# Rotating the queries of the first block's attention with SBUF transfers in place of a permutation matmul

## The chip, the cores and the metric

The kernel runs on one core of one Trainium2 chip. The metric is the device time of one execution in microseconds, over repeated executions. TensorE (PE) does the matmuls, VectorE (DVE) and ScalarE (ACT) the elementwise work, SyncE (SP) issues the weight transfers, and ACT issues the smaller ones.

## The reference, cut to what matters

Two blocks run one after the other on 256 tokens of width 2048, all in float32. The first block has two layers, and each layer has a sliding-window attention with 32 query heads of width 64, 4 key/value heads and a sink logit for each head. Per layer, the part around the change computes

```
q_b = rope(q_b.reshape(b, s, 32, 64), positions)      # 32 query heads
k_b = rope(k_b.reshape(b, s, 4, 64), positions)
o_b = swa_with_sinks(q_b, k_b, v_b, sinks).reshape(b, s, 2048) * silu(z_b)

def rope(x, positions):            # half = 32
    x1, x2 = x[..., :half], x[..., half:]
    return concatenate([x1 * cos - x2 * sin, x2 * cos + x1 * sin], -1)
```

In `rope` each half of a head's 64 numbers is needed beside the other half. In the attention, token i sees the keys j with 0 <= i - j < 128, in blocks of 128 tokens; the softmax takes the sink into its denominator. The columns `q_b` and `z_b` come out of the large projection `h @ w_in`. The rest (a gated delta rule before the attention, output projections after it, and the second block) is untouched.

## The kernel before, in words

**Weights.** Every projection is computed in blocks of 128 output columns. A block's weights (128 x 2048) are streamed from HBM into one of four slots of `raw` by SP. ACT rounds each half of a block to float32r (`Wh`, line 343, `act_cast`), DVE writes the remainder (`Wl`, line 349, `dve_low`), and PE multiplies a half as 8 x 3 matmuls of 256 columns (lines 278 to 280, `pe_half`). `Wh` and `Wl` have four places, so a cast into a place waits until PE has used the half that lay there, and the casts run four halves ahead of PE. The finished tile lies in bank `G[0]` or `G[1]`, and ACT copies it out (line 1625), which counts up `tile_taken`.

**Turns.** The attention stage (`pe_swa`, `act_swa`, `dve_swa`) runs in five turns per layer, g = 0 to 4; turns 1 to 3 are one rolled loop on each engine. A turn has 16 halves, n = 0 to 15. In turns 0 to 3 these are the blocks of the gate z (4 tiles, into `zx`) and of the queries q (4 tiles, into `qx`) of kv head g. In turn 4 they are the first 8 tiles of the next projection, whose tanh goes to `gm_more`. Between the halves of turns 1 to 4 lie the softmax steps of kv head c = g - 1 (`chain` is true). There are four query tiles t = 0 to 3 per kv head, with two heads in each, on partitions 0 to 63 and 64 to 127.

**Steps of tile t.** All three engines follow one order written out by hand. PE computes the scores ahead of half 4t + 1 (lines 1539, 1540). DVE adds the window mask and finds the maxima at n = 4t + 1 (lines 1656 to 1666). ACT does four exps at n = 4t + 2 (line 1597) and the sink's exp (line 1599). DVE normalises at n = 4t + 3 (lines 1670 to 1678). PE transposes the probabilities ahead of half 4t + 4 (line 1557), ACT copies them to `PT` (line 1604), and PE multiplies by the values ahead of half 4t + 5, behind the next scores (lines 1547 to 1549). DVE multiplies by the gate (line 1686), ACT rounds (line 1591) and DVE writes the low part (line 1693) at n = 4t + 6.

**The end of a turn.** Behind half 15 PE transposes for t = 3, then waits for ACT's copy of the last query tile and multiplies the four query tiles by the constant permutation `swap`, which exchanges rows i and i xor 32 (line 1572), and then does the value matmuls of t = 3. ACT copies the last tile (1625), makes the last cast (343), copies `PT` (1604), then the keys `kg` (1634). In the next turn it does the tanh of the gate (1587) and copies the values `vg` (1588). DVE does the last low part (349), multiplies the queries by the cosine (1710) and the permuted ones by the sine (1713), adds them (1716, step `turned`), finishes tile 3 (1686, 1693), and in the next turn makes the gate (1651). The first scores wait for `kg` and `turned`.

Of the kernel before, what the change touches and what calls it, by code (L numbers as in the profile page):

```python
# [21 lines left out]
ALU = mybir.AluOpType  # L22
# [3 lines left out]
P = 128  # L26
D = 2048
KT = D // P
T = 256
# [3 lines left out]
KV = 4  # L33
# [90 lines left out]
def build_program(nc, places, x_t, c_t, pos, stream, ada, ple_w, ple_x, rg_w, rpb, consts, params, params2, out_t, until=None):  # L124
    ctx = ExitStack()
    with ctx:
# [29 lines left out]
        B = PB[2:8]  # L156
# [63 lines left out]
        st_end = [stage("end_a", seeded=("dve",)), stage("end_b", seeded=("dve",))]  # L220
        st_y = stage("y")
        st_swa, st_rot = stage("swa"), stage("swa_turn")
        st_na, st_rgset, st_rg = stage("na"), stage("rgset"), stage("rg", seeded=("pe", "dve"))
        st_gu, st_zero, st_ple = stage("gu", seeded=("dve",)), stage("zero"), stage("ple")
        key_in, few_in = [sem(f"key_half_in{n}") for n in range(2)], sem("few_in")
# [1286 lines left out]

        qx, zx, qr, zsb = ws(0, 4, T), ws(1024, 4, T), ws(2048, 4, T), ws(3072, 4, T)
        Pm = [ws(4096, 2, 384), ws(4864, 2, 384)]
        qsin = ws(4096, 4, T)
        PT = ws(5632, 2, 384)
        kg, vg = ws(6400, T), ws(6656, 2, 64)
        of = ws(6784, T)
# [3 lines left out]
        def pe_swa(pe, l, g, chain):  # L1522
            S, q = st_swa, l * Q_LAYER + Q_PRE + Q_GDN + Q_END + 2 * g
            if chain:
                S.start("pe")
                c = g - 1
                r = l * KV + c

            def before(n):
                if n % 4 == 1 and n < 16:  # L1530
                    t = n // 4
                    if t == 0:
                        st_rot.wait(pe, "act", "kg", r)
                        st_rot.wait(pe, "dve", "turned", r)
                    else:
                        S.wait(pe, "dve", f"win{t - 1}", r)
                    for h in range(2):
                        hp = slice(64 * h, 64 * h + 64)
                        pe.matmul(B[h][:, 0:128], qr[hp, t, 0:128], kg[hp, 0:128], start=True, stop=True)
                        m = pe.matmul(B[h][:, 128:384], qr[hp, t, 128:256], kg[hp, :], start=True, stop=True)  # L1540
                    S.done(m, "pe", f"score{t}")
                if n % 4 == 1 and n > 1:
                    t = n // 4 - 1
                    S.wait(pe, "act", f"PT{t}", r)
                    for h in range(2):
                        hp = slice(64 * h, 64 * h + 64)
                        pe.matmul(B[4][hp, 0:P], vg[:, 0, :], PT[:, h, 0:P], start=True, stop=True)
                        pe.matmul(B[4][hp, P:2 * P], vg[:, 0, :], PT[:, h, P:2 * P], start=True, stop=False)
                        m = pe.matmul(B[4][hp, P:2 * P], vg[:, 1, :], PT[:, h, 2 * P:3 * P], start=False, stop=True)
                    S.done(m, "pe", f"pv{t}")  # L1550

                if n % 4 == 0 and n:
                    t = n // 4 - 1
                    S.wait(pe, "dve", f"prob{t}", r)
                    for h in range(2):
                        for x in range(3):
                            m = pe.transpose(B[2 + h][:, x * P:(x + 1) * P], Pm[t % 2][:, h, x * P:(x + 1) * P], ident)
                    S.done(m, "pe", f"turn{t}")

            for n in range(16):  # L1560
                if chain:
                    before(n)
                b, k = n // 2, n % 2
                pe_half(pe, q + b // 4, b % 4, k, l * TILES + 100 + g * 8 + b, b % 2, Hh, Hl)
            if isinstance(g, int) and g == KV:
                return before
            if chain:
                before(16)
            st_rot.start("pe")
            pe.wait_ge(tile_taken, l * TILES + 100 + g * 8 + 8 + 2)  # L1570
            for i in range(2):
                m = pe.matmul(B[i][:, :], const("swap"), qx[:, 2 * i:2 * i + 2, :], start=True, stop=True)
            st_rot.done(m, "pe", "swap")
            if chain:
                before(17)

        def act_swa(act, l, g, chain):
            S, q = st_swa, l * Q_LAYER + Q_PRE + Q_GDN + Q_END + 2 * g
# [5 lines left out]
            def work(n):  # L1584
# [15 lines left out]
                if n % 4 == 0 and n:  # L1600
# [3 lines left out]
                        x = act.copy(PT[:, h, :], B[2 + h][:, 0:384])  # L1604
                    S.done(x, "act", f"PT{t}")

            for n in range(16):
                if chain:
                    work(n)
                b, k = n // 2, n % 2  # L1610
                if n < 15:
                    act_cast(act, q + b // 4, b % 4, k)
                if k:
                    if chain and b == 0:
                        S.wait(act, "dve", "rot", r)
                    act_tile(act, q + b // 4, b % 4)
                    if b == 0:
                        act.wait_ge(tile_taken, l * TILES + 100 + g * 8 + 2)
                    if isinstance(g, int) and g == KV:
                        act.activation(gates8[:, b, :], G[b % 2][:, 0:T], ACT.Tanh, scale=0.5).then_inc(tile_taken, 1)  # L1620
                        if n == 15:
                            act_cast(act, q + 1, 3, 1)
                        continue
                    dst = zx[:, b, :] if b < 4 else qx[:, b - 4, :]
                    act.copy(dst, G[b % 2][:, 0:T]).then_inc(tile_taken, 1)
                    if n == 15:
                        act_cast(act, q + 1, 3, 1)
            if not isinstance(g, int) or g < KV:
# [9 lines left out]
        def dve_swa(dve, l, g, chain):  # L1638
# [6 lines left out]
            def before(n):  # L1645
                t = n // 4
                if n == 0:

                    st_rot.wait(dve, "dve", "turned", r)
                    S.wait(dve, "act", "vg", r)  # L1650
                    S.done(dve.scalar_tensor_tensor(zsb, zsb, 1.0, zx, ALU.add, ALU.mult), "dve", "rot")
                if n % 4 == 1:
# [35 lines left out]
            def after(n):  # L1688
                if n % 4 == 2 and n > 2:
# [2 lines left out]
                    at = bass.ds(c * 4 + t, 1)  # L1692
                    S.done(dve.tensor_tensor(Ol[:, at, :].rearrange("p a b -> p (a b)"), of, Oh[:, at, :].rearrange("p a b -> p (a b)").bitcast(F32), ALU.subtract), "dve", f"lo{t}")

            for n in range(16):
                if chain:
                    before(n)
# [3 lines left out]
                    dve_low(dve, q + (n - late) // 8, (n - late) // 2 % 4, (n - late) % 2)  # L1701
                if chain:
                    after(n)
            if chain:
                dve_low(dve, q + 1, 3, 1)
            if not isinstance(g, int) or g < KV:
                R, turn = st_rot, l * KV + g
                R.start("dve")
                dve.wait_ge(tile_taken, l * TILES + 100 + g * 8 + 8 + 2)
                R.done(dve.tensor_tensor(qr, qx, ROPE[:, 0:1, :].to_broadcast([P, 4, T]), ALU.mult), "dve", "cos")  # L1710
                R.wait(dve, "pe", "swap", turn)
                for i in range(2):
                    R.done(dve.tensor_tensor(qsin[:, 2 * i:2 * i + 2, :], B[i][:, :].rearrange("p (a b) -> p a b", b=T),
                                             ROPE[:, 1:2, :].to_broadcast([P, 2, T]), ALU.mult), "dve", f"sin{i}")
                R.wait(dve, "dve", "sin1", turn)
                R.done(dve.tensor_tensor(qr, qr, qsin, ALU.add), "dve", "turned")
            if chain:
                before(18)
                after(18)

# [1118 lines left out]
```

## Time and profile before

| | |
|---|---|
| time, median of 3 runs | 3941.32 us (3936.63 to 3944.15) |
| the profiled execution: span of its records (no other time of it is given) | 3936.2 us |
| PE busy | 3791.8 us (96%) |
| DVE busy | 2786.2 us (71%) |
| ACT busy | 1888.4 us (48%) |
| all DMA engines, mean rate | 182 GB/s |
| one attention turn, from the last transposes of turn 2 to those of turn 3 (layer 0) | 59.16 us, PE busy 59.16 |
| permutation matmuls (line 1572) | 32 instructions, 592 ns median |

The span is counted from the first to the last instruction. Matmul records overlap each other, so the distance between starts, not the duration, tells what a matmul costs PE. A busy share of PE near 1 means that hardly any time is left between records.

### The profile page before, as it was taken

What the parts mean: (1) busy time and instruction counts of PE and PEld (TensorE: products, weight loads), DVE (VectorE), ACT (ScalarE), POOL (GpSimd) and SP (SyncE); (2) the same over time, 40 slices, a digit from 0 to 9 for tenths busy, and PEclk for the clock granted to TensorE, in tenths of its full rate; (3) what the DMA queues carried; (4) which work ended last, traced back from release to release, by engine and by line L of the source; (5) the groups of instructions that cost most, each with busy time, mean ns of one, the idle gap of its engine ahead of it and who ended that gap; (6) DMA issues with size and microseconds to landing.
All of it is one profiled execution on the core that took longest, in us unless ns stands there. A gap on an engine that the chain in (4) does not pass through costs nothing.

```text
span 3936.2 us, 73085 instructions
## 1 busy us (share of the span) xinstructions
PE 3791.8 (96%) x28822; PEld 3598.6 (91%) x28822; DVE 2786.2 (71%) x3780; ACT 1888.4 (48%) x2849; POOL 185.9 (5%) x188
## 2 busy tenths in 40 slices
PE   1999999999999999999999999999999999999998
PEld 1999999999999999999999999999988798989888
DVE  7788887757777778888675675565576666666676
ACT  1546455335544355555533554454565433334365
POOL 0111211000000012121000000000000000000000
PEclk8999999999999999999999999999999999999999
DMA  9533433863368843434385434445534445555543
GB/s 396 182 141 138 143 135 141 304 220 142 140 236 311 297 148 139 144 138 147 139 317 198 140 140 169 182 162 179 187 111 168 171 171 193 182 183 183 182 149 129
DMA packets 137169, 716.41 MB, mean 182 GB/s; under 512 B 37184, under 2 KB 37632, under 8 KB 60800
## 3 DMA queue, kind: packets, MB, share of 16 engines
q1 hardware_dynamic: 111456, 631.31, 44.6%
q10 hardware_dynamic: 25504, 82.13, 5.9%
q8 instruction: 154, 2.52, 0.2%
q14 instruction: 55, 0.45, 0.0%
HBM read 711.22 MB, written 2.16 MB: 181 GB/s over the span
## 4 chain that ended last, share of the span: by engine, by line
PE 84%; DVE 7%; ACT 4%; issue 3%; DMA 2%; DVEq 0%; ACTq 0%; SPq 0%
PE bank L278 17%; PE bank L280 17%; PE bank L279 17%; PE bank L295 8%; PE bank L296 4%; PE bank L2346 2%; PE bank L2348 2%; PE bank L317 2%; PE bank L2347 2%; ACT Wh L343 2%; PE bank L321 2%; DMA raw<-in_ada 1%; DVE Wl L349 1%; PE bank L319 1%; PE bank L320 1%
## 5 line engine op out<-in xcount | busy, mean ns | idle before, releaser
L343 ACT CAST Wh<-raw 128x1024 fp32r<-128x1024 f32 x1124 | 1169.1, 1047 | 1664.1 <-PE bank L280 1226.0
L349 DVE TENSOR_TENSOR Wl<-raw,Wh 128x1024 fp32r<-128x1024 f32 x1124 | 1383.0, 1235 | 788.9 <-ACT Wh L343 784.1
L278 PE MATMUL bank<-H,Wh 128*128 128x256 f32 x5440 | 1597.0, 294 | 2.0 <-DVE Wl L349 1.2
L279 PE MATMUL bank<-H,Wh 128*128 128x256 f32 x5440 | 1538.4, 283 | 0.0
L280 PE MATMUL bank<-H,Wl 128*128 128x256 f32 x5440 | 1538.0, 283 | 0.0
L278 PEld LDWEIGHTS bank<-H,Wh 128*128 128x128 f32 x5440 | 1041.9, 192 | 29.2 <-issue 17.5
L279 PEld LDWEIGHTS bank<-H,Wh 128*128 128x128 f32 x5440 | 1042.5, 192 | 11.3 <-issue 8.6
L280 PEld LDWEIGHTS bank<-H,Wl 128*128 128x128 f32 x5440 | 1041.5, 191 | 0.0
L295 PE MATMUL bank<-H,Wh 128*128 128x512 f32 x1280 | 449.9, 396 | 6.4 <-DVE WS L336 6.1
L296 PE MATMUL bank<-H,Wl 128*128 128x256 f32 x1280 | 358.6, 280 | 0.0
L295 PEld LDWEIGHTS bank<-H,Wh 128*128 128x128 f32 x1280 | 240.6, 188 | 66.2 <-issue 5.5
L278 PE MATMUL bank<-O,Wh 128*128 128x256 f32 x896 | 255.7, 285 | 1.5 <-DVE Y L1496 0.8
L279 PE MATMUL bank<-O,Wh 128*128 128x256 f32 x896 | 254.9, 285 | 0.0
L280 PE MATMUL bank<-O,Wl 128*128 128x256 f32 x896 | 254.9, 284 | 0.0
L296 PEld LDWEIGHTS bank<-H,Wl 128*128 128x128 f32 x1280 | 242.3, 189 | 0.0
L2346 PE MATMUL bank<-O,Wh 128*128 128x256 f32 x704 | 199.9, 284 | 2.8 <-DVE WS L336 2.8
L2347 PE MATMUL bank<-O,Wh 128*128 128x256 f32 x704 | 199.2, 283 | 0.0
L2348 PE MATMUL bank<-O,Wl 128*128 128x256 f32 x704 | 199.1, 283 | 0.0
L278 PEld LDWEIGHTS bank<-O,Wh 128*128 128x128 f32 x896 | 173.4, 193 | 2.4 <-DVE Wl L349 2.0
L279 PEld LDWEIGHTS bank<-O,Wh 128*128 128x128 f32 x896 | 173.5, 194 | 0.0
L280 PEld LDWEIGHTS bank<-O,Wl 128*128 128x128 f32 x896 | 173.4, 194 | 0.0
L321 PE MATMUL bank<-H,Wl 128*128 128x256 f32 x576 | 161.4, 280 | 0.0
(413 smaller groups left out, 4776.7 us busy)
## 6 DMA issues: line engine op xcount, KB each, us to landing
raw<-in_stream SPq DMA_DIRECT2D x560, 1024.0 KB, 4.8
WS<-in_ada ACTq DMA_DIRECT2D x94, 512.0 KB, 6.1
raw<-in_ada SPq DMA_DIRECT2D x32, 1024.0 KB, 7.6
gm_more<-in_ada ACTq DMA_DIRECT2D x20, 512.0 KB, 6.9
WS<-rows_d ACTq DMA_DIRECT2D x16, 512.0 KB, 5.2
KR<-in_ada ACTq DMA_DIRECT2D x14, 512.0 KB, 6.9
raw<-in_stream SPq DMA_DIRECT2D x8, 512.0 KB, 6.8
X<-in_x_t SPq DMA_DIRECT2D x1, 2048.0 KB, 17.0
```

Of the source, the lines that this page charges most:

```text
L278: pe.matmul(out[:, 0:T], wh, xh[:, kt, :], start=first, stop=False)
L279: pe.matmul(out[:, 0:T], wh, xl[:, kt, :], start=False, stop=False)
L280: mm = pe.matmul(out[:, 0:T], wl, xh[:, kt, :], start=False, stop=last)
L295: pe.matmul(out[:, :], wh, x[:, kt, :, :], start=kt == 0, stop=False)
L296: mm = pe.matmul(out[:, 0:T], wl, x[:, kt, 0, :], start=False, stop=kt == KT - 1)
L317: pe.matmul(out[:, :], wh, x[:, kt, :, :], start=first, stop=False)
L321: mm = pe.matmul(out[:, 0:T], wl, x[:, kt, 0, :], start=False, stop=last)
L343: act.copy(Wh[:, n % 4, :], raw[:, (sbk + 2) % 4, k * (D // 2):(k + 1) * (D // 2)]).then_inc(hi_ready, 1)
L349: dve.tensor_tensor(Wl[:, n % 4, :], raw[:, (sbk + 2) % 4, k * (D // 2):(k + 1) * (D // 2)], Wh[:, n % 4, :].bitcast(F32), ALU.subtract).t ...
L2346: pe.matmul(o, wh, ah, start=x == 0, stop=False)
L2347: pe.matmul(o, wh, al, start=False, stop=False)
L2348: m = pe.matmul(o, wl, ah, start=False, stop=x == 3)
```

## The change

The permutation matmuls go. For each pair of query tiles (x = 0: tiles 0 and 1; x = 1: tiles 2 and 3) ACT issues four SBUF-to-SBUF transfers, of 32 partitions by 512 numbers each (64 KB), from `qx` into `qs`, which lies in `gm_more`. ACT does this behind its copies of blocks 5 and 7, which are n = 11 and n = 15, once its own copy is complete. DVE rotates pair 0 at n = 14 of the same turn, and pair 1 at n = 2 of the next turn; each has three operations of 128x512. The first scores of a turn wait for pair 0 alone, those of tile 2 for pair 1. Half 0 of the next turn is issued at the end of a turn, and the value matmuls of tile 3 stand in the middle of it. All value matmuls alternate between the two heads. ACT gets two waits, at n = 13 of a turn with softmax steps and at n = 5 of turn 4, so that pair 1's buffers are free.

```diff
-        qsin = ws(4096, 4, T)
+        qs = ws(0, 4, T, of=gm_more)
@@ pe_swa, before(n)
-                        st_rot.wait(pe, "dve", "turned", r)
+                        st_rot.wait(pe, "dve", "turned0", r)
+                    if t == 2:
+                        st_rot.wait(pe, "dve", "turned1", r)
@@ value matmuls
+                    halves = [slice(64 * h, 64 * h + 64) for h in range(2)]
                     for h in range(2):
-                        hp = slice(64 * h, 64 * h + 64)
-                        pe.matmul(B[4][hp, 0:P], vg[:, 0, :], PT[:, h, 0:P], start=True, stop=True)
-                        pe.matmul(B[4][hp, P:2 * P], vg[:, 0, :], PT[:, h, P:2 * P], start=True, stop=False)
-                        m = pe.matmul(B[4][hp, P:2 * P], vg[:, 1, :], PT[:, h, 2 * P:3 * P], start=False, stop=True)
+                        pe.matmul(B[4][halves[h], 0:P], vg[:, 0, :], PT[:, h, 0:P], start=True, stop=True)
+                    for h in range(2):
+                        pe.matmul(B[4][halves[h], P:2 * P], vg[:, 0, :], PT[:, h, P:2 * P], start=True, stop=False)
+                    for h in range(2):
+                        m = pe.matmul(B[4][halves[h], P:2 * P], vg[:, 1, :], PT[:, h, 2 * P:3 * P], start=False, stop=True)
@@ end of pe_swa
-            st_rot.start("pe")
-            pe.wait_ge(tile_taken, l * TILES + 100 + g * 8 + 8 + 2)
-            for i in range(2):
-                m = pe.matmul(B[i][:, :], const("swap"), qx[:, 2 * i:2 * i + 2, :], start=True, stop=True)
-            st_rot.done(m, "pe", "swap")
-            if chain:
-                before(17)
+            pe_half(pe, q + 2, 0, 0, f0 + 8, 0, Hh, Hl, between=(lambda: before(17)) if chain else None)
@@ act_swa
+            def swap(x):
+                act.wait_ge(tile_taken, l * TILES + 100 + g * 8 + (4 + 2 * x + 1 + 3))
+                for quarter in range(4):
+                    to, of_ = 32 * quarter, 32 * (quarter ^ 1)
+                    act.dma_start(qs[to:to + 32, 2 * x:2 * x + 2, :], qx[of_:of_ + 32, 2 * x:2 * x + 2, :]).then_inc(turned_in[x], 16)
...
+                    if isinstance(g, int) and g == KV and b == 2:
+                        st_rot.wait(act, "dve", "turned1", r)
...
+                    if b == 6 and chain:
+                        st_rot.wait(act, "dve", "turned1", r)
                     dst = zx[:, b, :] if b < 4 else qx[:, b - 4, :]
                     act.copy(dst, G[b % 2][:, 0:T]).then_inc(tile_taken, 1)
+                    if b == 5:
+                        swap(0)
+                    if b == 7:
+                        swap(1)
                     if n == 15:
                         act_cast(act, q + 1, 3, 1)
@@ dve_swa
+            def rotated(x, turn):
+                R, two = st_rot, slice(2 * x, 2 * x + 2)
+                dve.wait_ge(turned_in[x], 64 * turn + 64)
+                R.done(dve.tensor_tensor(qr[:, two, :], qx[:, two, :], ROPE[:, 0:1, :].to_broadcast([P, 2, T]), ALU.mult), "dve", f"cos{x}")
+                R.done(dve.tensor_tensor(qs[:, two, :], qs[:, two, :], ROPE[:, 1:2, :].to_broadcast([P, 2, T]), ALU.mult), "dve", f"sin{x}")
+                R.wait(dve, "dve", f"sin{x}", turn)
+                R.done(dve.tensor_tensor(qr[:, two, :], qr[:, two, :], qs[:, two, :], ALU.add), "dve", f"turned{x}")
...
                 if chain:
                     after(n)
+                if chain and n == 2:
+                    rotated(1, r)
+                if n == 14 and not (isinstance(g, int) and g == KV):
+                    st_rot.start("dve")
+                    rotated(0, l * KV + g)
             if chain:
                 dve_low(dve, q + 1, 3, 1)
-            if not isinstance(g, int) or g < KV:
-                R, turn = st_rot, l * KV + g
-                R.start("dve")
-                dve.wait_ge(tile_taken, l * TILES + 100 + g * 8 + 8 + 2)
-                R.done(dve.tensor_tensor(qr, qx, ROPE[:, 0:1, :].to_broadcast([P, 4, T]), ALU.mult), "dve", "cos")
-                R.wait(dve, "pe", "swap", turn)
-                for i in range(2):
-                    R.done(dve.tensor_tensor(qsin[:, 2 * i:2 * i + 2, :], B[i][:, :].rearrange("p (a b) -> p a b", b=T),
-                                             ROPE[:, 1:2, :].to_broadcast([P, 2, T]), ALU.mult), "dve", f"sin{i}")
-                R.wait(dve, "dve", "sin1", turn)
-                R.done(dve.tensor_tensor(qr, qr, qsin, ALU.add), "dve", "turned")
```

## Rows read from the trace of the kernel before

**Rows 1.** The page's busy times: engine, us, share of the span, instructions.

```profile
PE 3791.8 (96%) x28822; PEld 3598.6 (91%) x28822; DVE 2786.2 (71%) x3780; ACT 1888.4 (48%) x2849; POOL 185.9 (5%) x188
```

**Rows 2.** Busy times of one turn: stretch, length, PE, PEld, DVE, ACT, POOL, clock.

```profile
1003.36:1062.52 59.16, 59.16 (x495) 55.33 (x494) 41.97 (x86) 31.82 (x75) 0.00 (x0) 1.00 0.40 143
```

**Rows 3.** Timeline of PE, end of turn 2, layer 0: start, length, instruction.

```profile
1003.36 0.82 PE L1557 MATMUL bank<-C,WS 128*128 128x128 f32 x6
1004.01 1.96 PE L1572 MATMUL bank<-WS,C 128*128 128x512 f32 x4
1005.89 0.43 PE L1547 MATMUL bank<-WS 128*64 128x128 f32 x2
1006.17 0.32 PE L1547 MATMUL bank<-WS 128*64 128x128 f32 x1
1006.97 0.39 PE L278 MATMUL bank<-H,Wh 128*128 128x256 f32 x1
```

**Rows 4.** Timeline of ACT at the same place.

```profile
1003.55 0.37 ACT L1625 COPY WS<-bank 128x256 f32<-128x256 f32 x1 [1.34 <-PE bank L280]
1003.82 1.05 ACT L343 CAST Wh<-raw 128x1024 fp32r<-128x1024 f32 x1
1004.77 0.86 ACT L1604 COPY WS<-bank 128x384 f32<-128x384 f32 x2
```

**Rows 5.** Timeline of DVE and PE, start of turn 3, layer 0.

```profile
1009.64 0.42 DVE L1686 TENSOR_TENSOR WS<-bank,WS 128x256 f32<-128x256 f32 x1
1011.85 1.23 DVE L1651 SCALAR_TENSOR_TENSOR WS<-WS 128x1024 f32<-128x1024 f32 x1 [0.58 <-ACT WS L1588]
1017.85 0.16 DVE L1670 TENSOR_TENSOR WS<-WS 128x4 f32<-128x4 f32 x1
1018.46 1.01 DVE L1678 TENSOR_SCALAR WS<-WS 128x128 f32<-128x128 f32 x4
1019.63 0.82 PE L1557 MATMUL bank<-C,WS 128*128 128x128 f32 x6
```

**Rows 6.** Timeline of DMA issues of ACT that stand one behind another.

```profile
2811.74 0.34 ACTq L2056 DMA_DIRECT2D gm_more<-in_ple_w  x1
2813.86 0.67 ACTq L2056 DMA_DIRECT2D C<-in_ple_w  x1
139.03 0.87 ACTq L919 DMA_DIRECT2D rows_d<-WS  x2
```

**Rows 7.** Line 779's DMA issues: ns min/median/max; then its landing time.

```profile
L779 ACTq DMA_DIRECT2D WS<-in_ada x30: 334/334/653, 1133.1 to 1347.2; - x30
DMA to landing us min/median/max: 3.7/6.7/9.2
```

**Rows 8.** Timeline of DVE: the rotation's operations, end of turn 2, layer 0.

```profile
1006.04 1.22 DVE L1710 TENSOR_TENSOR WS<-WS,ROPE 128x1024 f32<-128x1024 f32 x1
1007.18 1.28 DVE L1713 TENSOR_TENSOR WS<-bank,ROPE 128x512 f32<-128x512 f32 x2
```

**Rows 9.** Timeline of DVE, n = 14 and 15 of turn 2, layer 0.

```profile
1000.02 0.42 DVE L1693 TENSOR_TENSOR O<-WS,O 128x256 f32 x1
1001.31 0.16 DVE L1670 TENSOR_TENSOR WS<-WS 128x4 f32<-128x4 f32 x1 [0.88 <-ACT WS L1599]
```

**Rows 10.** Timeline, end of turn 0 and start of turn 1, layer 0.

```profile
885.50 0.37 ACT L1625 COPY WS<-bank 128x256 f32<-128x256 f32 x1 [1.77 <-PE bank L280]
887.98 0.29 ACT L1588 COPY WS<-VB 128x128 f32 x1
891.81 1.23 DVE L1651 SCALAR_TENSOR_TENSOR WS<-WS 128x1024 f32<-128x1024 f32 x1
901.32 0.82 PE L1557 MATMUL bank<-C,WS 128*128 128x128 f32 x6
```

**Rows 11.** Timeline, n = 12 and 13 of turn 2, layer 0.

```profile
990.48 0.86 ACT L1604 COPY WS<-bank 128x384 f32<-128x384 f32 x2
993.54 0.43 PE L1547 MATMUL bank<-WS 128*64 128x128 f32 x2
```

More of the change, by code:

```diff
@@ L222, in build_program @@
         st_swa, st_rot = stage("swa"), stage("swa_turn")
+        turned_in = [sem(f"turned_queries{x}_in") for x in range(2)]
         st_na, st_rgset, st_rg = stage("na"), stage("rgset"), stage("rg", seeded=("pe", "dve"))
@@ L1558, in before @@
                     S.done(m, "pe", f"turn{t}")
-            for n in range(16):
+            f0 = l * TILES + 100 + g * 8
+            if not chain:
+                pe_half(pe, q, 0, 0, f0, 0, Hh, Hl)
+            for n in range(1, 16):
                 if chain:
@@ L1563, in pe_swa @@
                 b, k = n // 2, n % 2
-                pe_half(pe, q + b // 4, b % 4, k, l * TILES + 100 + g * 8 + b, b % 2, Hh, Hl)
+                pe_half(pe, q + b // 4, b % 4, k, f0 + b, b % 2, Hh, Hl)
             if isinstance(g, int) and g == KV:
@@ L1647, in before @@
                 if n == 0:
-                    st_rot.wait(dve, "dve", "turned", r)
+                    st_rot.wait(dve, "dve", "turned0", r)
                     S.wait(dve, "act", "vg", r)
@@ L1703, in dve_swa @@
                     after(n)
+                if chain and n == 2:
[3 more added lines that the diff above has]
+                    rotated(0, l * KV + g)
             if chain:
                 dve_low(dve, q + 1, 3, 1)
-            if not isinstance(g, int) or g < KV:
-                R, turn = st_rot, l * KV + g
-                R.start("dve")
-                dve.wait_ge(tile_taken, l * TILES + 100 + g * 8 + 8 + 2)
-                R.done(dve.tensor_tensor(qr, qx, ROPE[:, 0:1, :].to_broadcast([P, 4, T]), ALU.mult), "dve", "cos")
-                R.wait(dve, "pe", "swap", turn)
-                for i in range(2):
-                    R.done(dve.tensor_tensor(qsin[:, 2 * i:2 * i + 2, :], B[i][:, :].rearrange("p (a b) -> p a b", b=T),
-                                             ROPE[:, 1:2, :].to_broadcast([P, 2, T]), ALU.mult), "dve", f"sin{i}")
-                R.wait(dve, "dve", "sin1", turn)
-                R.done(dve.tensor_tensor(qr, qr, qsin, ALU.add), "dve", "turned")
-            if chain:
                 before(18)
```

## The prediction

> **What bounds the kernel now.** I read the page's busy times first: PE is busy for 3791.8 of 3936.2 us, DVE for 71%, ACT for 48% [rows 1]. PE sets the time, so a change is worth what it takes from PE's queue or adds to it as waiting. Next I read one turn as a stretch: PE is busy for all of its 59.16 us, at a granted clock of 1.00 [rows 2]. The timeline of PE at a turn's end shows the order: transposes at 1003.36, permutation at 1004.01, value matmuls at 1005.89, next half at 1006.97, without a gap [rows 3]. The permutation costs 1005.89 - 1004.01 = 1.88 us of PE.
>
> The other engines are not far behind, and that is the point of this case. At the start of a turn DVE is never idle from its step at 1009.64 but for short waits on ACT, its normalisation ends at 18.46 + 1.01 = 1019.47, and PE needs the result at 1019.63 [rows 5]. The slack is 0.16 us. Whatever is put into this chain of DVE delays PE nearly one for one.
>
> **What goes.** There are 8 turn ends, 4 per layer: 8 x 1.88 = 15.0 us of PE [rows 3]. In the two turn ends that follow turn 0, PE also waited for `turned`; that is part of the sum for turn 0 below.
>
> **The DMA issues on ACT.** ACT waits for its own copy (I take 0.1 us), issues four transfers, and only then makes the cast, the `PT` copies and `kg`. One issue takes 334 ns at least [rows 7], so four cost 1.34 us or more. Issued in a row they cost more: four of five took 2813.86 - 2811.74 = 2.12 us, and two small ones (16 KB each) took 0.87 [rows 6]. Twice 0.87 and a gap of 0.1 make 1.85; I take 1.9, since the small ones are nearest in size, and 0.1 until the next instruction. The ends 1.34 and 2.12 are kept for the range.
>
> **The end of turns 1 to 3.** ACT's copy ends at 1003.92 [rows 4]. The issues begin at 1004.0 and the cast at 1006.0. From the cast to the `PT` copies ACT needs 1004.77 - 1003.82 = 0.95 and for the copies 0.86 [rows 4], so `PT` is complete at 1007.8, and the value matmuls, which wait for it in the middle of half 0, start at 1007.9. Before, they started at 1005.89 [rows 3]. The permutation had covered the copy of `PT`; with it gone, `PT` is what is late. PE has used 1.5 us of this time for the first part of half 0 and stands still for the rest.
>
> DVE's next step (line 1686) can start when the value matmuls are complete, 1.08 + 0.1 behind their start [rows 3], at 1009.08. Before, it stood behind the rotation and started at 1009.64 [rows 5]: it is 0.56 earlier. From there to the end of the normalisation DVE needed 1019.47 - 1009.64 = 9.83 us [rows 5]. All those steps stay, and pair 1's rotation is put between them. Its three operations are 128x512: two such took 1.28 together, and one of 128x1024 took 1.22, twice as large [rows 8]. That makes 0.6 + 0.7 + 0.6 = 1.9. So the normalisation ends at 1009.08 + 9.83 + 1.9 = 1020.8, and the transposes come at 1020.85 where they came at 1019.63: 1.2 us later per such turn end, in spite of the missing permutation. ACT's exps don't bind there: they follow the maxima as before and end ahead of the rotation.
>
> Pair 0's rotation at n = 14 is mostly hidden. DVE is free at 1000.44 and waits 0.88 for ACT [rows 9]; with 1.9 put there, the normalisation starts at 1002.35 and takes 1.62, so the transposes at 1003.36 slip by about 0.6. The value matmuls wait for ACT until 1007.9 anyway, and ACT's chain starts from half 15. So this costs nothing as long as the issues take over about 0.4 us.
>
> The four issues at n = 11 stand ahead of the `PT` copies of tile 2, which began at 990.48 [rows 11]. They now begin at 992.7 and end at 993.55, where PE wants them at 993.54 [rows 11]: 0.1 us lost, and from here on every further tenth counts.
>
> Three such ends per layer: 3 x (1.2 + 0.1) = 3.9 us lost.
>
> **The end of turn 0.** There are no softmax steps. The copy ends at 885.50 + 0.37 = 885.87 [rows 10]; the issues and waits take 2.1 us, and the cast had started 0.1 ahead of the copy's end, so ACT's next steps move by 2.2. `vg`, complete at 888.27 before [rows 10], is complete at 890.47. DVE's gate step then starts at 890.5 (before: 891.81, behind the rotation [rows 10]). From the gate to the normalised tile DVE needs 1019.47 - 1011.85 = 7.62 [rows 5], and 1.9 for pair 1: 900.0. The transposes start at 900.1 instead of 901.32 [rows 10]: 1.2 us gained per layer.
>
> **The order of the value matmuls.** There are 32 groups of 1.08 us. The second head's first pass starts 1006.17 - 1005.89 = 0.28 behind the first head's, and then both heads overlap [rows 3]. With the heads alternating, the second can start at most 0.28 sooner. It may gain nothing if the passes are bound otherwise. I take 0.15, half way, since no row shows this order: 16 x 0.15 = 2.4 us gained per layer, bounds 0 and 4.5. The Trainium skill (TensorEngine Tiling (Array Packing), Key Properties) says that different tiles of the array can load weights and multiply in parallel; the overlap of the two heads in rows 3 agrees. By that rule taken fully the whole 0.28 would be gained, and the sum would be 4 us lower.
>
> **The rest.** The new waits of ACT on pair 1 (n = 13, and n = 5 in turn 4) come eleven and three halves behind the step at n = 2 that they wait for; the cast, copy and exps queued behind them are not held, so nothing. SP's queue is not touched; the transfers add 8 x 64 KB per turn to engines that are half idle.
>
> **Sum.** Per layer -1.2 + 3.9 - 2.4 = +0.3, both layers +0.6 us on the profiled 3936.2. The median of the runs lies 5.1 above that span (start, end and spread of runs). Forecast: 3942 us, no change.
>
> **Rivals.**
>
> *The issues don't hold up ACT.* The Trainium skill (DMA: Bandwidth & Descriptors, Issuing engines are not separate DMA queues) calls the sequencer's time to initiate a DMA usually small relative to the DMA itself. As a mechanism here: ACT's arithmetic goes on while the issues run. Then `PT` is complete at 1005.63 [rows 4] and the value matmuls start at 1006.2, bound by PE. DVE continues at 1007.4, the tile is normalised at 1007.4 + 9.83 + 1.9 = 1019.1, and each of the six ends gains 0.5. At turn 0 the gate starts at 888.3, the transposes at 897.9: 3.4 gained. Per layer -3.4 - 1.5 - 2.4 = -7.3, in all -14.6: 3927 us. This is nearly the whole permutation. For it: DMA issue has records of its own. Against it: issues in a row take 0.45 to 0.67 each [rows 6], and they are in ACT's program order, ahead of the cast.
>
> *The issues are slow* (slower). At the end of a turn and at n = 12 ACT stands between two PE steps. If each issue costs as the fifth in a row, 0.67 [rows 6], four with gaps take 2.9: 1.0 more at eight ends and six times at n = 12, +14 us: 3956 us. Slower by over 0.2% begins at about 2.4 us for four. For it: the fifth issue and the longest of line 779, 653 ns [rows 7]. Against: these moved 128 KB or more each, and the small pair did not take as long.
>
> *The transfers land late* (slower). Pair 0 has 1000.4 - 992.6 = 7.8 us from the last issue to its use, pair 1 has 11 us. Landing took 3.7 to 9.2 us for 512 KB from HBM [rows 7]. If they take 9.8 us, pair 0 comes 2 us late and holds DVE and then PE at tile 3's transposes, some 1.5 us in each of six turns: 3951 us. It decides from a landing of 7.8 us. Against it: 64 KB is an eighth of that size.
>
> **Chances.** Forecast 0.65, no hold-up by issues 0.19, slow issues 0.12, late landing 0.04. No measurement of this kernel tells under 0.2% (7.9 us) from no change. The forecast's own spread is: issues 1.34 to 2.12 (-4.5 to +3.1), alternating order (+4.8 to -4.2), rotation of 1.7 to 2.1 us (1.6 either way), runs (4 either way). It gives 0.56 same, 0.05 faster, 0.04 slower. With the rivals: faster 0.24, same 0.56, slower 0.20. The range 3931 to 3952 takes in that spread and part of the first rival's, and leaves out about 0.2.
>
> **What would show it.** In the trace after: four DMA issues in 1.9 us between ACT's copy and its cast at each turn end; PE idle ahead of the value matmuls in the middle of half 0, released by the `PT` copy, some 1.5 us; PE idle ahead of the first transposes of a turn, released by DVE's normalisation, about 0.9 us; those transposes 1.2 us later in distance from half 15's end than the 16.4 before; value matmul groups of 0.93 us. The prediction is wrong if the cast starts right behind the copy, if the first transposes don't wait for DVE, or if the issues take over 2.4 us.

## The result, and the profile after

The changed kernel took 3957.41 us (median of 7 runs, 3954.76 to 3961.84) beside 3944.15 for the kernel before on the same chip: ratio 1.0034, 95% interval 1.0025 to 1.0044, so 10 to 17 us slower. Forecast was no change, with 3931 to 3952. The profiled span is 3954.5 us.

The page's busy times of the changed kernel: PE is busy for 3.4 us less than in [rows 1], although the kernel is longer. PE waits instead.

```profile
PE 3788.4 (96%) x28790; PEld 3597.8 (91%) x28790; DVE 2788.4 (71%) x3796; ACT 1888.5 (48%) x2849; POOL 185.4 (5%) x188
```

The timeline of the changed kernel at the end of turn 2 of layer 0, the place of [rows 3] and [rows 4]. L1562 are the transposes, L1613 the transfers, L344 the cast, L1606 the `PT` copies, L1550 the first value matmuls, L1542 the next turn's first scores.

```profile
1005.17 0.37 ACT L1637 COPY WS<-bank 128x256 f32<-128x256 f32 x1 [1.33 <-PE bank L281]
1005.58 2.44 ACTq L1613 DMA_DIRECT2D gm_more<-WS  x4
1005.58 0.87 PE L1562 MATMUL bank<-C,WS 128*128 128x128 f32 x6 [0.44 <-DVE WS L1694]
1008.11 1.04 ACT L344 CAST Wh<-raw 128x1024 fp32r<-128x1024 f32 x1 [2.57 <-issue]
1009.06 0.85 ACT L1606 COPY WS<-bank 128x384 f32<-128x384 f32 x2
1009.97 0.44 PE L1550 MATMUL bank<-WS 128*64 128x128 f32 x4 [2.09 <-ACT WS L1606]
1013.74 0.61 PE L1542 MATMUL bank<-WS 64*128 64x128 f32 x4
```

The reader is to see three things. Four transfers keep ACT from its cast for 2.57 us. PE then stands idle for 2.09 us ahead of the value matmuls. And from the value matmuls to the next scores it takes 3.77 us for 12 value passes and 12 full-size matmuls. The last point is explained by the stretches below: length, busy PE, PEld, DVE, ACT and POOL, then the granted clock, and last the DMA engines' busy share and GB/s.

```profile
1005.50:1007.90 2.40, 2.30 (x18) 2.10 (x18) 1.15 (x2) 0.04 (x1) 0.00 (x0) 1.00 0.44 143
1007.90:1009.97 2.07, 0.00 (x1) 0.00 (x1) 0.78 (x1) 1.86 (x4) 0.00 (x0) 1.00 0.26 63
1010.90:1013.74 2.84, 2.84 (x14) 2.62 (x12) 1.29 (x3) 1.63 (x3) 0.00 (x0) 0.50 0.65 231
1015.00:1020.00 5.00, 5.00 (x44) 5.00 (x44) 4.44 (x9) 2.11 (x7) 0.00 (x0) 1.00 0.00 0
```

Behind the idle stretch the granted clock is 0.50, that is 1.2 GHz, until the scores, and then 1.00 again. Twelve matmuls take 2.84 us at this level, where 1.44 is usual.

Now the start of turn 3, the place of [rows 5]: L1702 is the finish of tile 3, L1667 the gate, L1714 and L1717 the first and last operation of pair 1's rotation, L1694 the normalisation.

```profile
1011.08 0.42 DVE L1702 TENSOR_TENSOR WS<-bank,WS 128x256 f32<-128x256 f32 x1 [0.67 <-PE bank L1554]
1013.30 1.23 DVE L1667 SCALAR_TENSOR_TENSOR WS<-WS 128x1024 f32<-128x1024 f32 x1 [0.57 <-ACT WS L1590]
1014.85 1.02 DVE L1672 TENSOR_TENSOR WS<-bank,C 128x384 f32<-128x384 f32 x2 [0.32 <-PE bank L1543]
1020.12 0.68 DVE L1714 TENSOR_TENSOR WS<-WS,ROPE 128x512 f32<-128x512 f32 x1
1021.44 0.69 DVE L1717 TENSOR_TENSOR WS<-WS,gm_more 128x512 f32<-128x512 f32 x1
1022.65 1.01 DVE L1694 TENSOR_SCALAR WS<-WS 128x128 f32<-128x128 f32 x4
1023.72 0.88 PE L1562 MATMUL bank<-C,WS 128*128 128x128 f32 x6
```

From one turn's last transposes to the next one's first it is 1023.72 - 1005.58 = 18.14 us, against 1019.63 - 1003.36 = 16.27 before [rows 3, 5]. Between one tile's transposes and the next the same subtraction gives, for the four quarters of a turn (us):

| kernel | t3 to t0 (turn end) | t0 to t1 | t1 to t2 | t2 to t3 |
|---|---|---|---|---|
| before | 16.27 | 14.30 | 14.29 | 14.30 |
| changed | 18.14 | 14.07 | 14.00 | 15.14 |

Five of the changed kernel's six turn ends take 18.14 to 18.21 us, one takes 17.27. All six have a wait of 2.09 to 2.11 us on PE; the granted clock falls behind five of them and stays at 1.00 behind the one of 17.27.

The table is the whole case. The two middle quarters gained 0.23 to 0.29 us. The quarter with pair 0's issues and rotation lost 0.84, and the turn end lost 1.87. The quarter from t2 to t3 contains this wait at n = 13 (place of [rows 11]); the other 0.44 us of it stand at the transposes in the first timeline above:

```profile
991.98 2.44 ACTq L1613 DMA_DIRECT2D gm_more<-WS  x4
994.53 0.86 ACT L1606 COPY WS<-bank 128x384 f32<-128x384 f32 x2 [2.58 <-issue]
995.44 0.44 PE L1550 MATMUL bank<-WS 128*64 128x128 f32 x4 [0.46 <-ACT WS L1606]
```

At the end of turn 0 (place of [rows 10]) nothing was gained: from ACT's copy to the first transposes 900.98 - 885.20 = 15.78 us, before 901.32 - 885.50 = 15.82. PE waits there for `kg`, behind the issues, and DVE's gate step (L1667) starts 5.47 us behind the start of ACT's copy, since the tanh and `vg` of ACT stand behind the issues too:

```profile
889.63 0.50 PE L1542 MATMUL bank<-WS 64*128 64x128 f32 x4 [1.60 <-ACT WS L1650]
890.67 1.22 DVE L1667 SCALAR_TENSOR_TENSOR WS<-WS 128x1024 f32<-128x1024 f32 x1 [0.23 <-ACT WS L1590]
899.91 1.01 DVE L1694 TENSOR_SCALAR WS<-WS 128x128 f32<-128x128 f32 x4
```

The granted clock in the stretch behind that wait is low too, 0.61 on the mean:

```profile
890.60:895.00 4.40, 4.40 (x25) 4.40 (x26) 4.09 (x9) 0.98 (x2) 0.00 (x0) 0.61 0.73 242
```

From that copy to the last transposes of turn 4, layer 0 took 245.80 us (before 239.97) and layer 1 245.11 (before 239.99). These 10.9 us are the change; the rest of the 13 is within the spread of the runs. The two profiled executions themselves differ by 18.3 us: the other 7.4 lie outside the attention turns, in work that the change leaves alone. From the last transposes of layer 0 to the turn 0 copy of layer 1, for instance, the thirteen profiled kernels take 1029.6 to 1039.4 us. So a single span is no measure of the change.

### The profile page after: what moved, and what is told of

The parts are those of the page before. It is cut to its first block, busy times and chain, and to the rows that moved or that the text cites. A ratio compares the mean times of both kernels' runs of the same rounds, so it can differ in the third digit from the quotient of the medians.

```text
span 3954.5 us, 73129 instructions
## 1 busy us (share of the span) xinstructions
PE 3788.4 (96%) x28790; PEld 3597.8 (91%) x28790; DVE 2788.4 (71%) x3796; ACT 1888.5 (48%) x2849; POOL 185.4 (5%) x188
## 4 chain that ended last, share of the span: by engine, by line
PE 81%; DVE 8%; ACT 4%; issue 4%; DMA 2%; ACTq 1%; DVEq 0%; SPq 0%
PE bank L279 17%; PE bank L281 16%; PE bank L280 16%; PE bank L296 8%; PE bank L297 4%; ACT Wh L344 2%; PE bank L2363 2%; PE bank L2365 2%; PE bank L2364 2%; PE bank L318 2%; PE bank L322 2%; DMA raw<-in_ada 1%; DVE Wl L350 1%; PE bank L320 1%; PE bank L321 1%
## 5 line engine op out<-in xcount | busy, mean ns | idle before, releaser
L344 ACT CAST Wh<-raw 128x1024 fp32r<-128x1024 f32 x1124 | 1169.1, 1047 | 1685.9 <-PE bank L281 1221.5
```

Of the source, the lines that this page charges most:

```text
L344: act.copy(Wh[:, n % 4, :], raw[:, (sbk + 2) % 4, k * (D // 2):(k + 1) * (D // 2)]).then_inc(hi_ready, 1)
```

## Experiments

Ratios are to the kernel before on the same chip, with 95% intervals. 1% is 39.4 us. The changed kernel stands at 1.0034. Each diff is against the changed kernel, unless the kernel before is named. "By the ratios" means the difference of two such ratios; the interval of a difference is wider than either.

**The order of the value matmuls alone**, on the kernel before.

```diff
-   for h in range(2): (three value matmuls of head h)
+   for h in range(2): (first) ; for h in range(2): (second) ; for h in range(2): (third)
```

> The kernel before with one part of the change alone: the value matmuls alternate between the two heads. Theory: this order is worth the difference between one turn's transposes and the next that the changed kernel shows in its undisturbed quarters, 14.00 us against 14.30, so 0.29 us for each of 32 groups: 9 us faster than before. Rival (the shorter quarters come from elsewhere in the change): no difference, within 2 us.

Measured: 0.9981 (0.9972 to 0.9990), 7.5 us faster. The quarters within a turn are 14.00 to 14.07 us against 14.29 to 14.30, the turn ends 16.11 to 16.22. So this part of the change is good, and, if the parts add up, the other parts together cost 0.34% + 0.19% = 0.53%, some 21 us.

**Useless matmuls in PE's idle time.**

```diff
-   between=(lambda: before(17)) if chain else None
+   between=(lambda: (pe_spin(pe, 4), before(17))) if chain else None
```

> The changed kernel with four useless matmuls of 256 float32 columns (some 1.9 us of PE) put into the middle of half 0 at the six ends of turns 1 to 3, just ahead of the wait for PT, where PE stood idle for 2.1 us. They write a bank that nothing reads. Theory: the idle time makes the chip lower PE's granted clock (0.50 in the stretch behind the wait), and the slow matmuls delay the first scores by 1.3 us and so DVE's chain by 0.8 us. Filled, the clock stays at 1.00 and the first transposes come 0.8 us earlier per turn end: 5 us faster than the changed kernel, so about 8 us slower than before. Rival (the clock falls for another reason, or its fall costs nothing since DVE sets the transposes): no difference from the changed kernel, 13 us slower than before; and if the useless work isn't hidden, up to 12 us slower still.

Measured: 1.0014 (1.0005 to 1.0023), 8 us faster than the changed kernel by the ratios. The same place in this kernel, first as a timeline (L331 is the useless work, L1702 and L1694 are DVE's finish of tile 3 and its normalisation), then the stretch from the value matmuls to the scores with its granted clock:

```profile
1011.37 1.89 PE L331 MATMUL bank<-C 128*128 128x256 f32 x8
1013.62 0.44 PE L1550 MATMUL bank<-WS 128*64 128x128 f32 x4 [0.35 <-ACT WS L1606]
1014.63 0.42 DVE L1702 TENSOR_TENSOR WS<-bank,WS 128x256 f32<-128x256 f32 x1 [0.56 <-PE bank L1554]
1016.04 0.50 PE L1542 MATMUL bank<-WS 64*128 64x128 f32 x4
1025.39 1.01 DVE L1694 TENSOR_SCALAR WS<-WS 128x128 f32<-128x128 f32 x4
```

```profile
1013.62:1016.04 2.42, 2.42 (x24) 2.12 (x24) 1.06 (x3) 1.11 (x3) 0.00 (x0) 1.00 0.31 54
```

The value matmuls start as late as in the changed kernel (1013.62 - 1009.23 = 4.39 us behind the transposes; there 1009.97 - 1005.58 = 4.39), but the clock stays at 1.00 and the way to the scores takes 2.42 us instead of 3.77. The turn ends take 17.06 to 17.28 us, where five of six took 18.14 or more. DVE's way from its finish of tile 3 to the normalised tile shows the same: 1026.40 - 1014.63 = 11.77 us here, 1023.66 - 1011.08 = 12.58 in the changed kernel. More work, less time: the lower clock is a cost of its own, and idle time brought it. The same execution has the comparison: at its two ends of turn 0 nothing was filled in, PE waits 1.60 us, and the clock falls behind both.

**Pair 1's issues behind `kg`.**

```diff
-                    if b == 7:
-                        swap(1)
...
                 st_rot.done(act.copy(kg, ...), "act", "kg")
+                swap(1)
```

> The changed kernel with pair 1's four transfers issued behind ACT's cast, PT copies and kg instead of ahead of them. Theory: the issues (2.45 us of ACT) ahead of the PT copies are what PE waits for in half 0. Behind them, the value matmuls don't wait and the clock stays at 1.00 there; the issues now delay ACT's rounding of the last tile, and DVE with pair 1's rotation in its chain normalises the first tile at about 16.5 to 17 us behind the last transposes (changed kernel: 18.15, before: 16.28), so PE waits there instead. About 1.6 us per turn end and 3 us at each turn 0: 12 to 16 us faster than the changed kernel, about the time of before. Rival (pair 1's rotation at n = 2 is the cause, the issues are hidden): less than 3 us faster than the changed kernel.

Measured: 0.9973 (0.9963 to 0.9983), 24 us faster than the changed kernel by the ratios, and beyond my bound: faster than before. The end of turn 2:

```profile
1001.92 0.87 PE L1562 MATMUL bank<-C,WS 128*128 128x128 f32 x6 [0.44 <-DVE WS L1693]
1002.96 0.51 ACTq L1613 DMA_DIRECT2D gm_more<-WS  x1
1003.21 0.49 ACT L1606 COPY WS<-bank 128x384 f32<-128x384 f32 x1
1003.58 0.42 ACT L1648 COPY WS<-KR 128x256 f32 x1
1004.15 0.44 PE L1550 MATMUL bank<-WS 128*64 128x128 f32 x4
1016.99 0.87 PE L1562 MATMUL bank<-C,WS 128*128 128x128 f32 x6 [0.65 <-DVE WS L1693]
```

The value matmuls don't wait. The issues begin at 1002.96, ahead of the second `PT` copy in time although they stand behind it in the program: arithmetic already handed to ACT runs on beside them. Turn ends are 14.91 to 15.13 us. My 16.5 to 17 had let the issues delay the rounding of tile 3, which did not happen. What remains is the 0.65 us wait for DVE.

**Pair 1's rotation at n = 3.**

```diff
-                if chain and n == 2:
+                if chain and n == 3:
                     rotated(1, r)
```

> The changed kernel with pair 1's rotation on DVE at n = 3, behind the first tile's normalisation, instead of n = 2 ahead of it. Theory: in the changed kernel PE, late from its wait and the low clock, reaches the first transposes only 0.1 to 0.2 us ahead of DVE, so this alone gains 1 to 3 us. Rival (the rotation in DVE's chain is the main cause): 0.9 us or more at each of eight turn starts, 7 to 10 us faster than the changed kernel.

Measured: 1.0025 (1.0014 to 1.0037), 3.5 us faster than the changed kernel, inside the intervals' width. Expected were 1 to 3, and 7 to 10 by the rival; the ratios do not decide between them. In the trace, the move takes only 0.2 us off the turn ends where the clock falls. The two attention stages together are 7.7 us shorter, but about 1.5 of these come from one more turn end at which the clock did not fall, and 3.7 from the two ends of turn 0, which take 14.03 and 14.06 us instead of 15.78 and 15.96: there too the clock stayed at 1.00 this time, behind waits of 1.59 and 1.62 us. Alone, this place is worth little. But this kernel shows the price of the clock cleanly, since DVE no longer sets the first transposes. Two turn ends of one execution, the first of layer 0 and the third:

```profile
949.77 0.44 PE L1550 MATMUL bank<-WS 128*64 128x128 f32 x4 [2.10 <-ACT WS L1606]
953.14 0.81 PE L1542 MATMUL bank<-WS 64*128 64x128 f32 x4
963.32 0.82 PE L1562 MATMUL bank<-C,WS 128*128 128x128 f32 x6
...
1071.94 0.44 PE L1550 MATMUL bank<-WS 128*64 128x128 f32 x4 [2.08 <-ACT WS L1606]
1074.38 0.50 PE L1542 MATMUL bank<-WS 64*128 64x128 f32 x4
1083.98 0.82 PE L1562 MATMUL bank<-C,WS 128*128 128x128 f32 x6
```

The same wait (2.10 and 2.08 us) is followed by 13.55 us to the transposes in one case and by 12.04 in the other, where the granted clock is 1.00 throughout. Four of the six turn ends take 17.87 to 17.96 us, two take 16.41 and 16.42. So the end with the fall of the clock is 1.5 us longer here.

**Both moves.** The diff is that of the last two together.

> The changed kernel with both moves: pair 1's transfers issued behind kg, and pair 1's rotation at n = 3. Theory: with the late issue alone PE waits 0.65 us for DVE at each first transposes of a turn (6.4 us in all); this wait goes, so 5 to 6 us faster than the late issue alone, some 16 us faster than before. Rival (what DVE does at n = 3 is then late for the halves or for the second tile): no faster than the late issue alone, 11 us faster than before.

Measured: 0.9952 (0.9939 to 0.9964), 19 us faster than before and, by the ratios, 8 us faster than with the late issues alone, where 5 to 6 were expected. Turn ends are 14.25 to 14.26 us, 0.66 to 0.87 less than with the late issues alone. With the issues ahead of the cast, the same move had taken only 0.2 us off the turn ends at which the clock fell (17.87 to 17.96 against 18.14 to 18.21): of two costs that lie beside each other, the smaller one shows only when the larger is gone.

**One transfer out of four.**

```diff
-                for quarter in range(4):
+                for quarter in range(1):
...
-                dve.wait_ge(turned_in[x], 64 * turn + 64)
+                dve.wait_ge(turned_in[x], 16 * turn + 16)
```

> The changed kernel with one of the four transfers of each pair; three quarters of the permuted queries are not written. Theory: the price is the number of issues on ACT (four take 2.44 us, one 0.6). The value matmuls then wait 0.2 us or less instead of 2.1, the granted clock stays at 1.00, the first transposes come 15.5 us behind the last ones of the turn before instead of 18.15: some 24 us faster than the changed kernel, 9 to 12 us faster than before. Rival (the transfers' data or ACT's wait for its own copy hold ACT, not the number of issues): within 5 us of the changed kernel.

Measured: 0.9965 (0.9952 to 0.9978), 27 us faster than the changed kernel by the ratios. One issue, `PT` ready early, then DVE's chain:

```profile
1001.02 0.51 ACTq L1613 DMA_DIRECT2D gm_more<-WS  x1
1003.49 0.44 PE L1550 MATMUL bank<-WS 128*64 128x128 f32 x4 [0.16 <-ACT WS L1606]
1016.32 0.88 PE L1562 MATMUL bank<-C,WS 128*128 128x128 f32 x6 [0.64 <-DVE WS L1694]
```

The wait is 0.16 us and the turn end 15.15 to 15.36, as expected. This run alone can't tell the number of issues from the amount of data, which is a quarter as well; the late issues above and SP's issues below move all the data and don't have the wait either, so it is ACT's time for the issues that costs.

**SP issues the transfers**, all else as in the changed kernel.

```diff
+            def swap(l, g, x):
+                sp.wait_ge(tile_taken, l * TILES + 100 + g * 8 + (4 + 2 * x + 1 + 3))
+                (the four dma_start of the changed kernel, on sp)
...
                     sp.dma_start(raw[:, s, :], stream[blocks + step * s]).then_inc(landed[s], 16)
+                    if behind and behind[0] == s:
+                        swap(*behind[1:])
```

> The changed kernel with all eight transfers of a turn issued by SP, between its weight transfers, and none by ACT; nothing else is moved, and pair 1's rotation stays at n = 2. Theory: ACT is free, no wait for PT, no lower clock; what is left is DVE's chain (transposes at 15.4 us instead of 16.28 in the kernel before) and 0.4 us at tile 3's transposes: 10 to 14 us faster than before. Rival (SP, held by its wait for the query tile and by eight issues of 0.6 us, is late with the weights): PE waits for Wl, no faster than before.

Measured: 0.9957 (0.9945 to 0.9969), 30 us faster than the changed kernel by the ratios. Turn ends 14.90 to 15.10. SP waits for the query tile at all 8 places of layer 0, 4.4 us at most, and PE's waits for `Wl` in that stage stay at the 0.7 us that the kernel before has too. That the issues stood in ACT's program is thus the cause from both sides.

**All moves.** Pair 0's issues behind the `PT` copies of n = 12, its rotation at n = 15 behind the normalisation, and the two moves above.

> The changed kernel with every move that the traces point to: pair 1's issues behind kg, pair 0's behind the PT copies at n = 12, pair 1's rotation at n = 3, pair 0's at n = 15 behind the normalisation. Theory: besides the gains of the two moves above, the 0.46 us wait for PT at n = 13 and the 0.44 us wait for tile 3's normalisation go, 0.9 us in six turns: some 21 us faster than before. Rival (pair 0's rotation at n = 15 delays DVE's last low part and the finish of tile 3, and so the next turn's first scores): no faster than the version with two moves.

Measured: 0.9947 (0.9934 to 0.9960), 21 us faster than before, as expected. No wait at the transposes is left. The four quarters of a turn are 14.01 + 14.01 + 14.00 + 14.35 = 56.37 us, with two moves they were 14.01 + 14.00 + 15.16 + 14.26 = 57.43: 1.06 us per turn, where 0.9 was expected. But turn 0 has no normalisation to hide behind, and its first scores now wait:

```profile
890.81 0.56 PE L1542 MATMUL bank<-WS 64*128 64x128 f32 x4 [1.72 <-DVE WS L1716]
```

**The kernel before without its permutation.**

```diff
-                m = pe.matmul(B[i][:, :], const("swap"), qx[:, 2 * i:2 * i + 2, :], start=True, stop=True)
...
-                    (sine times B[i])
+                    (sine times qx[:, 2 * i:2 * i + 2, :])
```

> The kernel before without the permutation matmuls; the sine is multiplied onto the unpermuted queries, so that the rotation is computed from the wrong half, and nothing else is changed or moved. Theory: the permutation's 1.88 us of PE per turn end lay beside ACT's cast and PT copies, which PE needs next (PT complete at 1005.63 where the permutation ended at 1005.89), so at six turn ends 0.2 us is gained and PE stands idle instead for 1.6 us, at a granted clock that may fall behind it; at the two ends of turn 0 DVE's rotation sets the first scores. In all 0 to 3 us faster than before, and if the clock falls, up to 6 us slower. Rival (the 15 us of PE are worth themselves): 13 to 17 us faster.

Measured: 1.0002 (0.9992 to 1.0012). This is the central test (0.8 us slower, with an interval of 3 faster to 5 slower). 15 us of PE work are gone and nothing is gained; PE waits in their place:

```profile
1007.19 0.82 PE L1557 MATMUL bank<-C,WS 128*128 128x128 f32 x6
1009.52 0.43 PE L1547 MATMUL bank<-WS 128*64 128x128 f32 x2 [1.51 <-ACT WS L1601]
```

Turn ends are 16.12 to 16.21 us against 16.27, with the clock at 1.00 behind the wait: there the copy of `PT` alone takes the gain away. At turn 0 the first scores wait 2.37 us for the rotation, where they waited 0.94, and the clock is 0.50 for 6.8 us behind it. From ACT's copy to the first transposes this end takes 18.71 us, before 15.82, in both layers. So 0.1 us is gained at each of six ends, and 2.9 is lost at each of the other two in this execution.

**All moves, turn 0 mended** (pair 0's rotation at n = 14 in turn 0).

> The version with all moves, but with turn 0 keeping pair 0's rotation at n = 14. Theory: in the version with all moves PE waits 1.7 us for this rotation at the first scores behind turn 0, and the granted clock falls there; with it gone the first transposes come some 4 us earlier in each layer: 8 us faster than the version with all moves, 28 us faster than before. Rival (this wait is replaced by that for kg): 3 us or less.

Measured: 0.9944 (0.9931 to 0.9958). From ACT's copy to the first transposes of turn 1 it is 899.07 - 886.70 = 12.37 us, against 901.93 - 886.25 = 15.68 without the mending. The trace gives 3.3 us per layer, where some 4 were expected, and PE's wait is gone; the ratios of the two versions, 0.9944 and 0.9947, differ by only 1 us and do not resolve the expected 8.

**SP's issues with all moves.**

> The version with SP's issues, with pair 1's rotation at n = 3 and pair 0's at n = 15 (n = 14 in turn 0). Theory: ACT has no issues at all, and DVE's chain is free as well, so this is the same as the version with all moves and turn 0 mended, within 2 us: 28 us faster than before. Rival (SP's issues take room from the weight transfers once PE runs without stalls): slower than that version by more than 3 us.

Measured: 0.9929 (0.9915 to 0.9942), 3916.78 us beside 3945.05. Quarters and turn ends are those of the version before it (14.01, 14.01, 14.00, 14.36); the intervals overlap. The two versions beat the kernel before by about 0.6 and 0.7%, and the changed kernel by 0.9 and 1.0%. Part of this, 0.19%, is the order of the value matmuls; the rest shows that the change's idea holds once its steps stand in other places.

## Why the prediction was wrong

Wrong in the time: 13 us slower, where no change was forecast and 3952 was the upper end. The slow rival had 3956 us, with 0.12. Its condition held: it decided from about 2.4 us for four issues, and four took 2.44. But its sum took 2.9 us for four; with 2.44 it gives 3942 + 14 x 0.54 = 3950. It was right by luck, since the clock stood in none of the terms.

Two steps of the prediction failed: the price of the issues, 1.9 us where four took 2.44, and the granted clock, which had no term at all. The attention stages were to become 0.6 us longer and became 10.9 longer. At each turn end with the quarter before it, 2.7 us were lost at five of six, where the prediction had 1.0 (1.2 + 0.1, less 0.15 for each of two groups of value matmuls); of the 1.7 between them, some 0.8 is the size of the issues (twice, n = 12 and turn end) and some 0.85 the clock.

- *What goes, 15.0 us of PE.* True as an amount, and worth nothing by itself: removed alone it gave 1.0002. The prediction had said that the permutation had covered the copy of `PT`; the run shows it.
- *The DMA issues, 1.9 us for four.* Mis-sized: 2.44 us, 514 ns for the first and 0.61 for the later ones. The small pair of [rows 6] was too cheap a model. At eight ends and six times at n = 12 the difference enters at once: the value matmuls of the turn end start 1009.97 - 1005.17 = 4.80 us behind the start of ACT's copy, where the prediction has 1007.9 - 1003.55 = 4.35. Issues of over 2.4 us were its own sign of being wrong.
- *The end of turns 1 to 3, +1.2.* The mechanism was right: PE idle ahead of the value matmuls in half 0 (forecast 1.5 us, measured 2.09), released by `PT`, and DVE's chain with 1.9 us of rotation setting the transposes (1020.12 to 1022.04 in the trace). From one turn's last transposes to the next one's first it was 18.14 us, where the prediction's own times give 1020.85 - 1003.96 = 16.9. PE's wait ahead of the first transposes, forecast at 0.9 us, was 0.10 to 0.17 at the five ends with the lower clock, since PE was late by itself, and 0.70 at the sixth.
- *The step that was missing.* No term had the granted clock, although the prediction itself had PE idle for some 1.5 us at six turn ends, and [rows 2] with its 1.00 spoke of a PE that never rests. At 0.50, twelve matmuls took 1.4 us more; the scores, then DVE's window step (0.32 us of waiting that was not there before) and its next low part (0.32 more) came later with them. From the finish of tile 3 to the normalised tile DVE took 12.58 us; the prediction has 9.83 + 1.9 = 11.73, and with the gap filled it was 11.77. So the chain was counted rightly for a clock of 1.00, and the clock is what it lacked. Filling the gap took 0.9 to 1.1 us off the five turn ends at which the clock had fallen.
- *The issues at n = 11, 0.1 us.* The wait was 0.46 us, by the size of the issue, and the quarter is 15.14 us with ACT's issues against 14.60 with SP's; "every further tenth counts" held.
- *Pair 0's rotation, 0.6 us, hidden.* The wait was 0.44 us, and the quarter is 14.60 with this rotation (SP's issues) against 14.01 with it at n = 15, so the 0.6 was right. Hidden at that place it was, behind the longer wait for `PT`; with the issues moved it became one of the last costs (the version with two moves against all moves).
- *The end of turn 0, 1.2 us gained.* 0.04 gained in layer 0, 0.13 lost in layer 1. The same two steps: DVE's gate step starts 5.47 us behind the copy's start instead of 5.0, by the size of the issues, and from there to the normalised tile it takes 900.92 - 890.67 = 10.25 us instead of 7.62 + 1.9 = 9.52, since the clock fell behind PE's 1.60 us of waiting for `kg`, a wait that the prediction did not have.
- *The order of the value matmuls, 4.8 us gained.* Measured 7.5, with an interval of 4 to 11. Within a turn it is 0.23 to 0.29 us per group, near the upper bound, and at the turn ends 0.05 to 0.16. The rule of the Trainium skill on tiles of the array (TensorEngine Tiling (Array Packing), Key Properties), taken fully, is thus the nearer one: the trace agrees with it within a turn.

The first rival (issues don't hold up ACT, 0.19) fell in the form it had: ACT waited 2.57 us with "issue" as the reason. The rule of the Trainium skill behind it (DMA: Bandwidth & Descriptors, Issuing engines are not separate DMA queues) says that the time to initiate a DMA is usually small relative to the DMA itself. Here one issue takes 0.61 us and its transfer lands in 2.1, and four in a row take longer than the landing. But behind queued arithmetic the issues did run beside it, as the version with late issues shows. The trace before had this already: at the place of [rows 6] a cast and a copy of ACT run while its issues are under way.

```profile
2811.70 1.05 ACT L343 CAST Wh<-raw 128x1024 fp32r<-128x1024 f32 x1 [2.45 <-PE bank L280]
2812.65 0.37 ACT L1941 COPY WS<-bank 128x256 f32<-128x256 f32 x1
```

What the issues hold up is the arithmetic that stands behind them in the program.

The third rival (late landing) fell: 1.9 to 6.7 us, median 2.1.

```profile
L1613 ACTq DMA_DIRECT2D gm_more<-WS x64: 514/612/1466, 875.1 to 2348.8; - x64
DMA to landing us min/median/max: 1.9/2.1/6.7
```

Open: why a wait of the same length lowered the clock at one place and not at another, in one execution too (five of six turn ends in the changed kernel, four of six with pair 1's rotation at n = 3).

## What to carry to other kernels

Before counting the work that a change takes from the bounding engine, ask what that work was covering: here 1.88 us of matmuls lay over work of ACT that PE then waited 1.5 us for, and taking them away alone gained nothing. A DMA issue is an instruction of the engine that issues it (0.5 to 0.6 us here); put it behind the last thing that somebody waits for, where queued arithmetic also hides it, or give it to an engine with time. And price a new wait of TensorE with the slower matmuls that may follow it.

## What the runs showed of the hardware that I had not expected

- In the attention stages of the profiled executions, 17 of 22 waits of 1.59 to 2.37 us on TensorE were followed by a granted clock of 0.50, for 3.4 us, and for 6.8 us behind the two of 2.37. None of the 8 waits of 1.37 to 1.51 us was. The place with the fall was up to 1.5 us longer than the same place without it. No threshold follows from this, since waits of about 1.6 and of 2.1 us stood on either side.
- Four 64 KB transfers inside SBUF take 2.44 us to issue in a row on ACT (3.33 and 4.17 for the first four of each layer in the changed kernel), 2.41 on SP, and one alone takes 0.51 on ACT.
- Value matmuls on the two column halves of the array, alternated, take 0.28 us less per group of twelve passes than head after head, within a turn.
